# Weight parts in one wide tile each: four buffers 8320 bytes apart, shifted by 4 bytes for every four chunks

## What is computed

```python
h = h + rms_norm(nsa_mixer(rms_norm(h)))    # sparse attention
h = h + rms_norm(conv_ffn(rms_norm(h)))     # up 1024 -> 2 x 2816, conv, silu * , down 2816 -> 1024
h = h + rms_norm(ssd_mixer(rms_norm(h)))    # state space scan
h = h + rms_norm(conv_ffn(rms_norm(h)))
h = h + rms_norm(gated_delta_and_memory(rms_norm(h), mem))
h = h + rms_norm(ffn(rms_norm(h)))
```

## Time and profile before

| | |
|---|---|
| median of 2 runs | 1200.83 us (1198.42 to 1203.24) |
| the profiled execution | 1198.59 us, span 1196.8 us, clock 0.999 |
| PE busy | 1169.6 us, 98% of the span, 9852 matmuls |
| DVE, ACT, POOL busy | 846.8, 651.5, 149.1 us |
| HBM traffic | 162 GB/s over the span |

### The profile page before, as it was taken

One profiled execution on the slowest core, in us unless ns is written; L12 is line 12 of the kernel. 1 busy time (PEld: TensorE's weight loads), 2 busy tenths in 40 slices (PEclk: granted clock), 3 DMA queues, 4 the chain that ended last, 5 costly groups with the idle time before them and its releaser, 6 DMA issues.

```text
span 1196.8 us, 23183 instructions
## 1 busy us (share of the span) xinstructions
PE 1169.6 (98%) x9852; PEld 1073.7 (90%) x9852; DVE 846.8 (71%) x1299; ACT 651.5 (54%) x1171; POOL 149.1 (12%) x143
## 2 busy tenths in 40 slices
PE   8899999999999899999999999999999999999998
PEld 8897789999889898978999988999989878999986
DVE  6678777888557988886788875857577776655542
ACT  4657556666446665645666663665435534645431
POOL 1220000000002332101000000103443311000000
PEclk9999999999999999999999999999999999999999
DMA  8832225555635443353655564442221322755540
GB/s 307 272 142 89 96 106 202 198 211 185 241 108 176 150 185 142 115 182 108 252 194 189 212 244 160 179 177 106 108 107 72 117 97 92 279 190 198 180 173 35
DMA packets 31622, 196.67 MB, mean 164 GB/s; under 512 B 4000, under 2 KB 5664, under 8 KB 9376
## 3 DMA queue, kind: packets, MB, share of 16 engines
q1 hardware_dynamic: 27504, 185.17, 43.1%
q10 hardware_dynamic: 4016, 10.03, 2.7%
HBM read 193.09 MB, written 1.05 MB: 162 GB/s over the span
## 4 chain that ended last, share of the span: by engine, by line
PE 87%; DVE 6%; ACT 3%; issue 2%; POOL 1%; DMA 0%; DVEq 0%; POOLq 0%; ACTq 0%
PE bank L539 24%; PE bank L541 23%; PE bank L540 23%; DVE wlo L528 2%; PE bank L1895 1%; PE bank L1133 1%; PE bank L1190 1%; PE bank L1217 1%; ACT whi L520 1%; PE bank L726 1%; PE bank L2539 1%; PE bank L3006 1%; POOL rr L668 1%; DVE xc L1602 1%; PE bank L2482 1%
## 5 line engine op out<-in xcount | busy, mean ns | idle before, releaser
L528 DVE TENSOR_TENSOR wlo<-raw,whi 128x1024 fp32r<-128x1024 f32 x322 | 388.6, 1244 | 88.3 <-ACT whi L520 87.7
L539 PE MATMUL bank<-xT,wlo 128*128 128x256 f32 x1488 | 417.8, 281 | 4.7 <-DVE xc L1602 2.5
L540 PE MATMUL bank<-xT,whi 128*128 128x256 f32 x1488 | 412.3, 277 | 0.0
L541 PE MATMUL bank<-xT,whi 128*128 128x256 f32 x1488 | 412.2, 277 | 0.0
L520 ACT ACTIVATE whi<-raw 128x1024 fp32r<-128x1024 f32 (+1 forms) x349 | 349.4, 1048 | 114.6 <-PE bank L541 83.2
L539 PEld LDWEIGHTS bank<-xT,wlo 128*128 128x128 f32 x1488 | 279.9, 188 | 8.4 <-DVE xc L1602 3.2
L540 PEld LDWEIGHTS bank<-xT,whi 128*128 128x128 f32 x1488 | 279.5, 188 | 0.6 <-issue 0.5
L541 PEld LDWEIGHTS bank<-xT,whi 128*128 128x128 f32 x1488 | 279.9, 188 | 0.0
L668 POOL TENSOR_TENSOR rr<-rr,nhalf 128x1 f32<-128x1 f32 x34 | 24.8, 730 | 706.0 <-DVE rr L656 518.9
L541 PE MATMUL bank<-whi,gT 128*128 128x512 f32 x264 | 103.9, 394 | 0.0
L540 PE MATMUL bank<-wlo,gT 128*128 128x512 f32 x264 | 103.3, 391 | 0.0
(11 more groups left out here) (390 smaller groups left out, 1761.7 us busy)
## 6 DMA issues: line engine op xcount, KB each, us to landing
raw<-in_wall SPq DMA_DIRECT2D x173, 1024.0 KB, 4.8
grow<-in_rows ACTq DMA_DIRECT2D x13, 512.0 KB, 5.5
h<-in_x SPq DMA_DIRECT2D x4, 256.0 KB, 5.5
dsk<-in_rows ACTq DMA_DIRECT2D x4, 256.0 KB, 3.2
memx<-in_mem ACTq DMA_DIRECT2D x1, 1024.0 KB, 10.9
out<-h SPq DMA_DIRECT2D x4, 256.0 KB, 2.0
masks<-in_masks SPq DMA_DIRECT2D x1, 580.0 KB, 12.9
D<-Tx ACTq DMA_DIRECT2D x4, 128.0 KB, 6.3
```

Of the source, the lines that this page charges most:

```text
L528: e.tensor_tensor(low, src, high, SUB).then_inc(*up("dve.low", p))
L539: e.matmul(out, a[1], b[0], start=start, stop=False)
L540: e.matmul(out, a[0], b[1], start=False, stop=False)
L541: return e.matmul(out, a[0], b[0], start=False, stop=stop)
```

## The change

`whi` and `wlo` become one wide tile each, in which buffer i % 4 begins every 2080 elements (8320 bytes) in place of 8192. Inside its place, chunk i begins (i // 4) % 32 elements further. So chunks 0 to 3 begin at 0, chunks 4 to 7 at 4 bytes, up to chunks 124 to 127 at 124 bytes; chunks 128 to 131 begin at 0 again, and the last, chunk 174, at 44 bytes. Everything that reads or writes weight parts takes its view from the new function `parts`. `raw` stays as it is. The tiles behind `wlo` lie 1024 bytes further, `xT` among them; this leaves their places modulo 128.

The room comes from `masks`, which loses the two 128 x 128 matrices. Their matmuls now read one column of `blk64` (column 384 or 511 of `masks`), repeated 128 times with a step of 0. Every tile behind `masks` lies where it was, so `gT`, `yT`, `yG`, `mT` and `X` do not move. The DMA of `masks` falls from 1160 to 904 columns. No instruction is added, taken away or moved: on each engine the list of instructions is the same, with the same shapes but for that DMA.

```diff
-_MASKS = 6 * 128 + 8 * 64 + 8
+_MASKS = 4 * 128 + 8 * 64 + 8
...
-    m = [r == c, r <= c, (r <= c) & same, same, (r < 64) & (c >= 0), (r >= 64) & (c >= 0)]
+    m = [r == c, r <= c, (r <= c) & same, same]
...
-        whi = [sb([128, 2048], f32r, name="whi") for _ in range(NHL)]
-        wlo = [sb([128, 2048], f32r, name="wlo") for _ in range(NHL)]
+        wparts = [sb([128, 2080 * NHL], f32r, name=n) for n in ("whi", "wlo")]
...
-        half = [masks[:, 512:640], masks[:, 640:768]]
+        half = [masks[:, c:c + 1].to_broadcast([128, 128]) for c in (384, 511)]
...
+        def parts(i):
+
+            o = 2080 * (i % NHL) + (i // NHL) % 32
+            return [w[:, o:o + 2048] for w in wparts]
+
         def wof(i):
 
-            return [w[i % NHL][:, 0:sizes[i]].rearrange("p (k n) -> p k n", k=plan[i][2]) for w in (whi, wlo)]
+            return [w[:, 0:sizes[i]].rearrange("p (k n) -> p k n", k=plan[i][2]) for w in parts(i)]
...
-            v = whi[i % NHL][:, 0:1024].rearrange("p (k n) -> p k n", k=8)
+            v = parts(i)[0][:, 0:1024].rearrange("p (k n) -> p k n", k=8)
...
-            return src, whi[i % NHL][:, o:o + w], wlo[i % NHL][:, o:o + w]
+            return (src, *(v[:, o:o + w] for v in parts(i)))
```

More of the change, by code:

```diff
@@ L329, in build @@
         ident, tri, tri64, blk64 = (masks[:, 128 * i:128 * i + 128] for i in range(4))
-        half = [masks[:, 512:640], masks[:, 640:768]]
-        level, (idc, tric) = ([masks[:, 768 + 64 * i:832 + 64 * i] for i in v] for v in (range(6), range(6, 8)))
+        half = [masks[:, c:c + 1].to_broadcast([128, 128]) for c in (384, 511)]
+        level, (idc, tric) = ([masks[:, 512 + 64 * i:576 + 64 * i] for i in v] for v in (range(6), range(6, 8)))
         ones1 = masks[:, 255:256]
-        own8 = masks[0:120, 1280:1288]
+        own8 = masks[0:120, 1024:1032]
         neg_qk, neg_sl, neg_gd = negb[:, 0:128], negb[:, 128:256], negb[:, 256:320]
```

## The result

The changed kernel takes 1218.91 us (1218.55 to 1219.28, 2 runs) against 1200.83 (1198.42 to 1203.24). The ratio is 1.014, with a 95% interval from 1.0092 to 1.0187: slower by 1.4%, surely slower, and less than 2%. The forecast of 1204 is missed by 15 us; the range from 1187 to 1224 holds it. (Two corrections to the text ahead of the prediction. There are 176 chunks, 0 to 175, and the last one, which begins at 44 bytes, is chunk 175. And of the 22 chunks of an up projection the first two are taken with the weights moving; the 20 after them, 960 matmuls, have the weights stationary.)

What follows compares the result with a forecast made beforehand. PE's matmul stream, busy 98% of the span, was taken as the bound; 0 + 0 + 0 + 3 us (matmul addresses) on 1196.8 plus 1.8 gave 1201.6, and 2.2 more for the median 1204, range 1187 to 1224.

Runs made afterwards that it cites:

- spacing: Changed kernel with the buffers still 8320 bytes apart and the shift gone; 1201.86 us, ratio 1.0032 to the kernel before.
- w32: Changed kernel with buffers 8192 bytes apart and every weight part 32 bytes further, activations unmoved; 1220.87 us, ratio 1.0156 to the kernel before.
- all32: As `w32`, but every tile behind the weights, all activations among them, also 32 bytes further; 1202.87 us, ratio 0.9988 to the kernel before.
- both4: Changed kernel with buffers 8192 bytes apart, all weight parts and `xT` 4 bytes further; 1239.07 us, ratio 1.0339 to the kernel before.
- both16: As `both4`, with weight parts and `xT` 16 bytes further in place of 4; 1199.47 us, ratio 0.9994 to the kernel before.
- x4: As `both4`, but the weights stay at 0 and `xT` alone is 4 bytes further; 1230.23 us, ratio 1.0234 to the kernel before.
- w44: Changed kernel with buffers 8192 bytes apart and every weight part 44 bytes further; 1229.35 us, ratio 1.0226 to the kernel before.
- w12: Changed kernel with buffers 8192 bytes apart and every weight part 12 bytes further; 1195.74 us, ratio 0.9975 to the kernel before.
- w24: Changed kernel with buffers 8192 bytes apart and every weight part 24 bytes further; 1203.92 us, ratio 1.0042 to the kernel before.
- mix: As `w12`, with `gT`, `yT`, `yG`, `mT` and `X` 32 bytes earlier and `xT` unmoved; 1195.56 us, ratio 0.9972 to the kernel before.

## What to carry to other kernels

Where PE's stream bounds a kernel, count its matmuls in 40 us before and after any change of the SBUF layout, even one that moves no instruction, for tiles that stood 4 to 44 bytes elsewhere made from -0.3% to +3.4% here. Try a few fixed offsets between the moving and the stationary tiles and keep the best; the two kernels with varied offsets got good and bad places mixed (+1.4 and +1.2%). A fixed offset is no gain by itself: four of those tried cost 1.6% or more, two gave 0.3%, and on so small a gain the steps between executions weigh heavily. A trace that holds a single placement bounds nothing for the others, and a range should then reach beyond the paces that it shows.

## What the runs showed of the hardware that was not expected

- An fp32r matmul stream at 2.4 GHz without waits has a pace that goes with the places of both operands: from 113.3 to 122.2 ns for 256 columns and from 226.7 to 240.0 for 512. Several of the paces are 3.33 ns or a multiple of it apart (113.3, 116.7, 120.0; 226.7, 233.3, 240.0), but 117.3, 118.7, 121.1 and 122.2 are not on that grid.
- What counts is the distance between the operands modulo 256 bytes (`spacing`, where buffers 128 bytes apart differ with 512 columns and buffers 256 bytes apart don't; `w32` against `all32`) and, below 16 bytes, where they stand themselves (`both4` against `both16`). Each was tried at one or two places only.
- ACT, DVE and POOL read and wrote the same shifted parts at no price.
- One placement can have two paces, and this is the rule more than the exception. The three up projections went at 113.3, 117.8 and 117.8 ns in `all32`, 117.3, 117.3 and 118.7 in `w32`, 122.2, 121.7 and 121.7 in `x4`, 120.0, 122.2 and 122.2 in `w44`, 120.0, 121.1 and 121.1 in `both4`. A stream may change its pace within its first 150 or so matmuls (in `spacing` from 117.8 to 113.3) and then keeps it to the end of the up projection. The steps of 4.2 us between executions of one program have the size of one up projection at 117.8 in place of 113.3.
- In the traces of `w12`, `w24`, `mix` and `both16` all three up projections are at 113.3 ns, and none of their 31 executions stands out by such a step. Beside them the kernel before had 2 in 17 executions on one chip and 3 in 9 on the other, so this is a sign and not a proof.

**What stays open.** That the reads of the moving operand and of the weights being loaded meet in the memory is argued from the fact that both places matter; no run shows it. Why one placement has two paces, and what chooses, was not found; the two values at the shift of 88 may be of the same kind. Since every pace comes from one trace of one execution, a place that showed one pace may have another. Nor is there a formula: 4 bytes for both operands cost 40 us, and nothing in the twelve runs would have foretold that number.
